# Rotary embedding in one stage: a 32-row shuffle on VectorE replaced by a rotation matmul on TensorE and a multiply on GpSimd

## The reference

```
def rms_norm(x, g):
    y = xf * lax.rsqrt(jnp.mean(xf * xf, axis=-1, keepdims=True) + EPS)
    return (y * g).astype(x.dtype)

def apply_partial_rotary(x, cos, sin):        # the first 32 of 128 channels of a head
    x1, x2 = x[..., :16], x[..., 16:32]
    rot = concatenate([x1 * cos - x2 * sin, x2 * cos + x1 * sin])
    return concatenate([rot, x[..., 32:]])

def mixer_b(h, w_in, q_gain, k_gain, w_out):  # 3 patterns g, 8 heads of 128 channels
    qkv = (h @ w_in)[..., :n_qkv] as (512, 3, 3, 8, 128);  z = the rest
    for g, (window, dilation) in enumerate(((128, 1), (512, 4), (2048, 16))):
        q = apply_partial_rotary(rms_norm(qkv[:, :, 0, g], q_gain[g]), cos, sin)
        k = apply_partial_rotary(rms_norm(qkv[:, :, 1, g], k_gain[g]), cos, sin)
        o, lse = dilated_window_attention(q, k, qkv[:, :, 2, g], window // dilation, dilation)
    wgt = softmax(stack(lses), axis=0)
    o = sum over g of wgt * o
    return (o * silu(z)) @ w_out
```

## Time and profile before

| | us |
|---|---|
| median of 3 runs | 3138.42 (3136.17 to 3145.52) |
| the profiled execution | 3136.17 |
| its span | 3134.3 |
| TensorE busy / VectorE busy / GpSimd busy | 2940.8 / 1774.4 / 269.2 |

### The profile page before, as it was taken

The page is one execution under the profiler, slowest core; times in us unless marked ns, Lnnn a source line. Parts: engine busy times, 40 slices in busy tenths (PEclk is TensorE's granted clock), DMA queues, the critical chain, the costliest instruction groups (busy, mean ns, idle before and its releaser), DMA issues.

```text
span 3134.3 us, 39236 instructions
## 1 busy us (share of the span) xinstructions
PE 2940.8 (94%) x14032; PEld 2416.0 (77%) x14032; DVE 1774.4 (57%) x2633; ACT 1107.3 (35%) x1620; POOL 269.2 (9%) x247
## 2 busy tenths in 40 slices
PE   8999999988999899999999988699999878899998
PEld 6888888877887678878888865488888744788887
DVE  5555536653576466654555586765344568464445
ACT  4332324443354432223422444443222423442222
POOL 1000000000000000000000061220000444010001
PEclk9999999999999899999999999699999988999999
DMA  4322322112211123223232321023222210122222
GB/s 141 108 91 84 108 88 68 61 54 68 75 55 61 54 97 99 95 94 97 85 101 87 104 69 44 14 75 108 96 98 94 88 34 14 41 89 99 96 99 87
DMA packets 70410, 252.22 MB, mean 80 GB/s; under 512 B 7808, under 2 KB 9856, under 8 KB 69632
## 3 DMA queue, kind: packets, MB, share of 16 engines
q1 hardware_dynamic: 68112, 241.89, 23.3%
q10 hardware_dynamic: 2160, 8.49, 0.8%
HBM read 248.25 MB, written 2.10 MB: 80 GB/s over the span
## 4 chain that ended last, share of the span: by engine, by line
PE 81%; DVE 8%; issue 4%; POOL 3%; ACT 2%; DMA 0%; DVEq 0%; ACTq 0%; POOLq 0%
PE ps L296 18%; PE ps L298 18%; PE ps L297 18%; PE ps L567 2%; PE ps L568 2%; PE ps L569 2%; PE ps L767 1%; POOL arena L1953 1%; PE ps L768 1%; PE ps L769 1%; PE ps L810 1%; PE ps L796 1%; DVE w_low L283 1%; PE ps L590 1%; PE ps L828 1%
## 5 line engine op out<-in xcount | busy, mean ns | idle before, releaser
L283 DVE TENSOR_TENSOR w_low<-raw,w_high 128x1024 fp32r<-128x1024 f32 x456 | 566.8, 1248 | 427.1 <-ACT w_high L276 417.8
L296 PE MATMUL ps<-h_high,w_high 128*128 128x512 f32 x1872 | 742.6, 397 | 26.3 <-DVE root L1001 10.2
L297 PE MATMUL ps<-h_low,w_high 128*128 128x512 f32 x1872 | 733.8, 392 | 0.0
L298 PE MATMUL ps<-h_high,w_low 128*128 128x512 f32 x1872 | 733.4, 392 | 0.0
L276 ACT ACTIVATE w_high<-raw 128x1024 fp32r<-128x1024 f32 x456 | 478.2, 1051 | 438.7 <-PE ps L298 214.3
L296 PEld LDWEIGHTS ps<-h_high,w_high 128*128 128x128 f32 x1872 | 354.9, 190 | 103.0 <-issue 28.5
L298 PEld LDWEIGHTS ps<-h_high,w_low 128*128 128x128 f32 x1872 | 354.6, 189 | 74.6
L297 PEld LDWEIGHTS ps<-h_low,w_high 128*128 128x128 f32 x1872 | 355.1, 190 | 70.9
L296 PE MATMUL ps<-y_high,w_high 128*128 128x512 f32 x688 | 270.4, 393 | 0.7 <-DVE y_low L1797 0.4
L297 PE MATMUL ps<-y_low,w_high 128*128 128x512 f32 x688 | 268.6, 390 | 0.0
L298 PE MATMUL ps<-y_high,w_low 128*128 128x512 f32 x688 | 268.4, 390 | 0.0
(11 more groups left out here) (391 smaller groups left out, 4577.8 us busy)
## 6 DMA issues: line engine op xcount, KB each, us to landing
raw<-stream SPq DMA_DIRECT2D x456, 512.0 KB, 3.4
table<-tables_in ACTq DMA_DIRECT2D x5, 1088.0 KB, 5.9
x<-x_in ACTq DMA_DIRECT2D x8, 256.0 KB, 8.4
x_out<-x SPq DMA_DIRECT2D x16, 128.0 KB, 1.7
const<-const_in SPq DMA_DIRECT2D x1, 673.0 KB, 8.3
work<-ssm_in ACTq DMA_DIRECT2D x1, 512.0 KB, 3.6
params<-params_in ACTq DMA_DIRECT2D x1, 287.0 KB, 6.8
```

The lines of the kernel that those rows point to most:

```text
L283: nc.vector.tensor_tensor(w_low[:, u.slot], raw[:, u.raw], w_high[:, u.slot].bitcast(F32), ALU.subtract).then_inc(weights_low, 1)
L296: nc.tensor.matmul(bank, wh, high[:, k], start=k == 0, stop=False)
L297: nc.tensor.matmul(bank, wh, low[:, k], start=False, stop=False)
L298: mm = nc.tensor.matmul(bank, wl, high[:, k], start=False, stop=k == tiles - 1)
```

## The change

The rotary step of stage b is written as stage e has it. For each of the 48 tiles:

- TensorE multiplies the whole tile with a constant 128x128 matrix that swaps and negates channels, into bank 3 of PSUM, right after the sums of squares (L803 of the changed kernel, semaphore `b_rot`). Bank 3 is also where kn spreads its factors, so the rotation matmul waits until VectorE has read what was there (`b_turned`, `b_k_done`), and kn waits for the slot's own `b_turned`.
- VectorE multiplies bank 3 with the sine (L938, 128 partitions, `b_turned`), and adds it to the tile (L941, `b_qk_done`) after GpSimd's part.
- GpSimd multiplies the tile with the cosine in place (L1015, new function `b_gpsimd`, `b_cosed`), after `b_rot`.
- The shuffle, the two multiplies on 32 partitions and the negation of the sine table are gone, and VectorE's wait for `b_gained` and the last tile's `b_qk_done` ahead of `split_low`.

```
@@ b_tensor, in the tile step, after the sums of squares
                         mm.then_inc(b_ss, 1)
+                        if n > 0:
+                            pe.wait_ge(b_turned, lin(n, i, 24))
+                        if tile[1] == 5 or (tile[1] == 0 and n > 0):
+                            done = 3 * tile[0] + 2 if tile[1] == 5 else 3 * tile[0]
+                            pe.wait_ge(b_k_done, lin(done, i, 12))
+                        if tile[1] == 4:
+                            pe.wait_ge(b_k_done, lin(3 * tile[0] + 1, i, 12))
+                        nc.tensor.matmul(ps[:, 3], con("rot_b", 0, P), b_tile(*tile), start=True,
+                                         stop=True).then_inc(b_rot, 1)
@@ b_tensor, in kn
-                        if 3 * j0 + g > 0:
-                            pe.wait_ge(b_k_done, lin(3 * j0 + g, i, 12))
+                        if u > 0:
+                            pe.wait_ge(b_turned, lin(6 * j + u, i, 24))
+                        else:
+                            pe.wait_ge(b_turned, lin(6 * j, i, 24))
@@ b_vector, in the slot
-                    if tile is not None:
-                        n = B_TILES * tile[0] + tile[1]
-                        dve.wait_ge(b_gained, lin(n + 1, i, 24))
-                        if n > 0:
-                            dve.wait_ge(b_qk_done, lin(n, i, 24))
                     if unit is not None:
                         split_low(dve, unit + AHEAD)
                     if tile is not None:
                         n = B_TILES * tile[0] + tile[1]
-                        nc.vector.stream_shuffle(b_t2, b_tile(*tile)[0:ROTARY], SWAP).then_inc(b_shuffled, 1)
-                        dve.wait_ge(b_shuffled, lin(n + 1, i, 24))
-                        nc.vector.tensor_tensor(b_t2, b_t2, b_sin, ALU.mult).then_inc(b_turned, 1)
-                        nc.vector.tensor_tensor(b_tile(*tile)[0:ROTARY], b_tile(*tile)[0:ROTARY], b_cos,
-                                                ALU.mult).then_inc(b_turned, 1)
-                        dve.wait_ge(b_turned, lin(2 * n + 2, i, 48))
-                        nc.vector.tensor_tensor(b_tile(*tile)[0:ROTARY], b_tile(*tile)[0:ROTARY], b_t2,
-                                                ALU.add).then_inc(b_qk_done, 1)
+                        dve.wait_ge(b_rot, lin(n + 1, i, 24))
+                        if n > 0:
+                            dve.wait_ge(b_qk_done, lin(n, i, 24))
+                        nc.vector.tensor_tensor(b_t2[:], ps[:, 3], b_sin, ALU.mult).then_inc(b_turned, 1)
+                        dve.wait_ge(b_turned, lin(n + 1, i, 24))
+                        dve.wait_ge(b_cosed, lin(n + 1, i, 24))
+                        nc.vector.tensor_tensor(b_tile(*tile), b_tile(*tile), b_t2[:], ALU.add).then_inc(b_qk_done, 1)
@@ new, called in GpSimd's list of stages at stage b
+        def b_gpsimd(pool):
+            pool.wait_ge(table_loaded, 16 * (TABLED.index("b") + 1))
+            with pool.Fori(0, 2) as i:
+                for j in range(BH):
+                    for n in range(B_TILES):
+                        pool.wait_ge(b_rot, lin(6 * j + n + 1, i, 24))
+                        nc.gpsimd.tensor_tensor(b_tile(j, n), b_tile(j, n), b_cos, ALU.mult).then_inc(b_cosed, 1)
```

More of the change, by code:

```diff
@@ L95 @@
 MASKED = -1.0e30
-ROTARY = 32
 class Unit:
@@ L232, in build @@
         b_v_copied, b_gained, b_ss = sem("b_v_copied"), sem("b_gained"), sem("b_ss")
-        b_shuffled, b_turned, b_qk_done = sem("b_shuffled"), sem("b_turned"), sem("b_qk_done")
-        b_signed = sem("b_signed")
+        b_rot, b_turned, b_cosed, b_qk_done = sem("b_rot"), sem("b_turned"), sem("b_cosed"), sem("b_qk_done")
         b_root_done, b_rk_done, b_rq_done = sem("b_root_done"), sem("b_rk_done"), sem("b_rq_done")
@@ L711, in build @@
         b_sq = (sq, ssq)
-        b_t2, b_szs, b_r = root[0:ROTARY], (sq, root), rstd
-        b_cos, b_sin = table[0:ROTARY, 0:T], table[0:ROTARY, T:2 * T]
+        b_t2, b_szs, b_r = root, (sq, root), rstd
+        b_cos, b_sin = table[:, 0:T], table[:, T:2 * T]
         b_strip = table[:, 2 * T:2 * T + 9 * P]
@@ L717, in build @@
         B_SOFT = 7
-        SWAP = [(m + ROTARY // 2) % ROTARY for m in range(ROTARY)]
         def b_tile(j, n):
@@ L901, in b_vector @@
             dve.wait_ge(table_loaded, 16 * (TABLED.index("b") + 1))
-            upper = b_sin[0:ROTARY // 2]
-            nc.vector.tensor_scalar(upper, upper, -1.0, None, op0=ALU.mult).then_inc(b_signed, 1)
-            dve.wait_ge(b_signed, 1)
             with dve.Fori(0, 2) as i:
@@ L2733, in _ @@
                 r = R_POST.get(name, None if last else R_PRE[name] + 1)
+                if name == "b":
+                    b_gpsimd(pool)
                 if name == "e":
```

## The result

The changed kernel takes 3190.65 us (median of 4 runs, 3184.71 to 3193.1) against 3138.08 us (3136.17 to 3145.52) before: a ratio of 1.0161, 95% interval 1.0139 to 1.0182. It is slower by 52.6 us by the medians, and by 50.5 us if one goes by the ratio. The profiled execution took 3185.59 us with a span of 3183.8, 49.5 us more span than before. In a second set of runs the median was 3188.39 us, 51 more than the kernel before beside it.

A forecast was written before the change was run, and what follows sets the result against it. TensorE was taken as the bound, full in the slots that the change touches. Terms of 41.3 + 6.1 + 0.6 = 48.0 us on the profiled 3136.2 give 3184.2; with the median 2.3 above that execution, 3186 us, range 3173 to 3202.

The forecast's parts named there:

- Term 1: Stage b, 48 tiles: TensorE pays 0.86 us for each rotation matmul, 41.3 us in all, bounds 38 to 46.
- Term 2: Slots (0, 4), (0, 5), (1, 0), both passes: kn waits for the sine multiply, 6 x 1.02 = 6.1 us, bounds 0 to 8.
- the case of the dropped clock: Rival, 4%: six new waits of about 1 us lower TensorE's clock, 15 us more, 3201 us.
- Term 3: Six u = 3 slots: GpSimd's multiply delays the copy TensorE's L832 waits for; 0.1 us each, 0.6 us, ends 0 and 5.5.
- the case of VectorE and GpSimd as the bound of the softmax slots: Rival, 5%: slow GpSimd multiplies make VectorE 0.7 us late in each of 24 slots, 17 us more, 3203 us.
- VectorE at nothing: Stage b's 48 tiles: VectorE's 66 us less busy time buys no TensorE time, so it is costed at nothing.
- The half-price case: Rival, 4%: the rotation matmul costs one piece instead of two, 27 us in all, 3165 us.

The follow-up runs named there:

- The matmul alone: The kernel before plus one unused float32 128x512 rotation matmul per tile ahead of the sums of squares, VectorE keeping the shuffle: 3181.91 us against 3138.78.
- GpSimd twice: The changed kernel with GpSimd's cosine multiply done twice in a row for every tile: 3200.3 us, 11.9 above the changed kernel on the same chip.
- half the columns: The changed kernel with the rotation matmul over 256 of the 512 columns: 3165.06 us, 23 to 26 less than the changed kernel.

## Why the prediction was right

The forecast was 3186 us within 3173 to 3202, and the first set gave 3190.65. The mechanism was the one that was foreseen: TensorE pays the matmul, kn's wait is added in six slots, and VectorE's saving earns nothing.

**Term 1** was the price of the matmul, 0.86 us a tile. The records in stage b are 96 as foreseen:

```profile
L803 PE MATMUL ps<-arena,const x96: 592/634/676, 474.2 to 1052.7; 128*128 128x512 f32 x96
```

The 634 is no length of any record. Each rotation has one piece of 676 ns, the first, and one of 592, where stage e had 590 for most. Yet the slots without attention work grew by 0.86 exactly. Behind the sums the rotation costs 0.94 (541.24 to 542.18 us), and the group behind it saves the 0.08 that it paid before; the text had taken that side of its bounds.

**Term 2** was 1.02 us in six slots; it measured 1.07 to 1.12 by the table, 6.5 us for 6.1. The timeline of slot (0, 4) of the changed kernel:

```profile
495.09 0.95 PE L793 MATMUL ps<-const,ssq 128*128 128x1 f32 x8
...
495.90 1.10 PE L803 MATMUL ps<-arena,const 128*128 128x512 f32 x2
...
497.05 0.69 DVE L938 TENSOR_TENSOR root<-ps,table 128x512 f32<-128x512 f32 x1 [2.55 <-PE ps L803]
497.09 1.27 POOL L1015 TENSOR_TENSOR arena<-arena,table 128x512 f32<-128x512 f32 x1 [5.93 <-PE ps L803]
...
497.87 1.15 PE L850 MATMUL ps<-const,arena 128*128 128x128 f32 x8 [0.86 <-DVE root L938]
498.46 0.69 DVE L941 TENSOR_TENSOR arena<-arena,root 128x512 f32<-128x512 f32 x1 [0.72 <-POOL arena L1015]
...
498.78 0.48 PE L294 MATMUL ps<-h_high,w_high 128*128 128x512 f32 x1
...
499.10 0.40 PE L295 MATMUL ps<-h_low,w_high 128*128 128x512 f32 x1
```

The sine multiply starts 1.15 us after the rotation, not 1.06, and kn at 1.97, not 1.88. Since kn would have started at 0.95 and not at 0.86, the two errors cancel and the start is late by the 1.02 us of the forecast. What the term left out is the 0.10 us that kn takes longer behind a wait. The clock did not fall: the first product record behind it (L294) is 0.48 us long and the next one 0.40, and the granted clock is 1.00 from 480 to 700 us, which holds the three waits of the first pass, and from 830 to 1050 us, which holds those of the second:

```profile
480.00:700.00 220.00, 217.57 (x1166) 176.69 (x1165) 109.21 (x188) 91.00 (x137) 29.31 (x23) 1.00 0.17 56
```

That answers the case of the dropped clock. The Trainium skill (TensorE: Matmul & The Clock Gate, "A second HAM failure mode: psum-queue depth-cycling") tells of short idle times between groups of matmuls that made the clock swing in another kernel. Six idle times of 0.8 to 0.9 us did not do so here.

**Term 3** was a tight fit that was to cost 0.1 us in six slots. Slot (1, 3) of the changed kernel:

```profile
540.42 0.95 PE L793 MATMUL ps<-const,sq 128*128 128x1 f32 x8
...
541.24 1.10 PE L803 MATMUL ps<-arena,const 128*128 128x512 f32 x2
...
543.81 0.69 DVE L941 TENSOR_TENSOR arena<-arena,root 128x512 f32<-128x512 f32 x1 [0.73 <-POOL arena L1015]
...
544.42 0.16 DVE L945 SCALAR_TENSOR_TENSOR arena<-ps,norm_col 128x12 f32<-128x12 f32 x1
...
544.73 0.37 ACT L889 ACTIVATE work<-ps 128x256 f32<-128x256 f32 x1
...
545.15 0.71 PE L838 MATMUL ps<-arena 128*128 128x128 f32 x4
```

The copy L889 ends at 545.10 and L838 starts at 545.15, 4.73 us after the sums, 0.07 later than the prediction's 4.66. The slot grew by 0.93 instead of 0.86, the same 0.07, some 0.4 us in six slots for 0.6. One reading behind this term was wrong, though, and that the number came out is in part luck. The prediction took 3.80 us as the time at which TensorE by itself comes to the second part of the scores, with the copy done 0.05 before. But 0.05 us is what passes between the copy's end and the start that it releases, in the changed kernel as well: TensorE was already waiting for that copy. In the kernel without rotary work, where the copy is early, L832 starts 3.75 us after the sums and takes 0.37 us to the next product instead of 0.47:

```profile
529.06 0.95 PE L796 MATMUL ps<-const,sq 128*128 128x1 f32 x8
...
532.81 0.61 PE L832 MATMUL ps<-arena 128*128 128x128 f32 x4
...
533.18 0.48 PE L296 MATMUL ps<-h_high,w_high 128*128 128x512 f32 x1
```

The matmul alone gives the same: without any wait for the copy the slot would be 10.52 - 0.86 = 9.66 us long, and it was 9.84 before. So the chain over the copy costs 0.2 us a slot in the changed kernel, most of which the kernel before paid too.

Why the chain kept to its short form is GpSimd's time:

```profile
L1015 POOL TENSOR_TENSOR arena<-arena,table x48: 1261/1273/1301, 475.4 to 1053.3; 128x512 f32<-128x512 f32 x48
```

All 48 multiplies took 1.26 to 1.30 us, none the 1.64 or 2.28 of stage e. Of VectorE's instructions only the sine multiply, which reads one operand from PSUM, ran beside them, and the subtract was over at least 0.84 us before each. By the Trainium skill (SBUF — State Buffer, "Who interferes with whom") a VectorE instruction with two SBUF inputs gets in the way of a GpSimd one that reads SBUF, and one with a single SBUF input does not. These 48 agree with the second half, and the six multiplies of 1.58 us in the run with GpSimd twice with the first, though they were 0.31 us longer for a subtract that ran 0.45 us beside them.

The run with GpSimd twice shows how tight the fit is: of the extra 1.27 us per multiply the u = 3 slots hid next to nothing, all others everything. It also speaks against the case of VectorE and GpSimd as the bound of the softmax slots: there 1 us more of GpSimd's time was to cost some 0.7 us in each of 24 slots, and 1.27 us more cost nothing but in the six u = 3 slots.

**VectorE at nothing** holds within 3 us, by the run without its rotary work. The half-price case is refuted by the 0.86 us of the matmul alone and the 0.43 us of half the columns.

The sum by the trace is 41.3 + 6.5 + 0.4 = 48.2 us against 47.9 measured in the stage. The medians' 51 to 53 us are 3 to 5 more. The profiled execution of each kernel lies below its median (by 1.9 and 5.1 us in the first sets), and the runs of the changed kernel fall into two groups, which the granted clock tells apart: 3183.7 to 3185.7 us at a mean of 0.964 to 0.966, and 3189.9 to 3193.1 us at 0.961 to 0.962. The kernel before has such groups too, 3134.9 to 3139.4 and 3142.0 to 3145.5 us, with the clock less cleanly apart. The median depends on how many runs fell into which. A shift of this size is enough for the 4.7 us between forecast and result; the sum had no term for it, and only the width of the range took it in. What decides the clock of a run is open.

## What to carry to other kernels

Work may go to the engine that is full only if it takes more from it than it brings; moving work off an engine with idle time can buy next to nothing, here at most 3 us for 126 us of work. Price such a change by two things, the time from start to start of the new instruction on the full engine, and each place where the full engine must wait for a reader of the same PSUM bank with nothing between. The list of waits of the full engine names what is really to be won: here an order of two VectorE steps in four slots, 17 to 19 us. Where the gain is a few us, compare the length of the changed stage in two profiles before the medians of whole programs.

## What the runs showed of the hardware

- A float32 matmul of 128x512 costs 0.86 us and one of 128x256 0.43 us of TensorE's time at the granted clock of 1.00, though their records last 1.02 to 1.10 and 0.68 us in sum. Behind single-column matmuls the first of the two records is 676 ns long instead of 590 and the pair costs 0.94, and its successor 0.08 less.
- The list of waits understates a wait behind a long matmul record: 0.86 us in the list were 1.12 us of slot length. Of the difference 0.15 is the record's tail (1.10 us long, while the next group can start at 0.95) and 0.10 is that the group behind the wait takes longer: kn 0.91 us instead of 0.81, the second part of the scores 0.47 instead of 0.37.
- Six GpSimd multiplies of 128x512 float32 that ran beside the last 0.45 us of a VectorE subtract of two SBUF operands took 1.58 us instead of 1.27. Six that met the last 0.12 us of one were not delayed.
- After much the same waits of up to 5.1 us the stretch at the lower clock was not equally long in all kernels: mean clock 0.82 over the end of the first pass of the changed kernel (703 to 754.5 us), 0.73 with GpSimd twice (707 to 760 us).
- The same 9050 matmul records behind the stage took 2073.0 us at a mean clock of 0.96 in one execution and 2078.3 us at 0.95 in another.
